# Layer norm statistics on VectorE, the last two experts one by one, and the last norm and store in halves

## The reference

```python
def layer_norm(x, g, b):
    xf = x.astype(jnp.float32)
    mu = jnp.mean(xf, axis=-1, keepdims=True)
    var = jnp.mean(jnp.square(xf - mu), axis=-1, keepdims=True)
    return ((xf - mu) * lax.rsqrt(var + EPS) * g + b).astype(x.dtype)
...
        h = layer_norm(DEEPNORM_ALPHA * h + mix, ln_g[layer, 0], ln_b[layer, 0])
        ffn = peer(h, peer_w_q[layer], peer_subkeys[layer], peer_u[layer], peer_v[layer])
        h = layer_norm(DEEPNORM_ALPHA * h + ffn, ln_g[layer, 1], ln_b[layer, 1])
```

```python
        act = jax.nn.gelu(jnp.einsum('td,ted->te', xb, u), approximate=False)
        coef = (gate * act.astype(jnp.float32)).astype(xb.dtype)
        return jnp.einsum('te,ted->td', coef, expert_v[e])
```

## Time and profile before

| | |
|---|---|
| median of 3 runs | 2472.62 us (2468.64 to 2475.14) |
| the profiled execution | 2467.16 us, of which the span of instructions is 2465.4 us |
| busy: TensorE, VectorE, ScalarE, GpSimd | 90%, 68%, 37%, 35% of the span |
| DMA | 939.16 MB, 805.36 MB of it gathers of experts |
| bandwidth in most of the stream | 425 to 427 GB/s |
| mean granted TensorE clock | 0.987 of full speed |

### The profile page before, as it was taken

The page is one execution under the profiler, slowest core; times in us unless marked ns, Lnnn a source line. Parts: engine busy times, 40 slices in busy tenths (PEclk is TensorE's granted clock), DMA queues, the critical chain, the costliest instruction groups (busy, mean ns, idle before and its releaser), DMA issues.

```text
span 2465.4 us, 29977 instructions
## 1 busy us (share of the span) xinstructions
PE 2215.2 (90%) x9826; PEld 1270.1 (52%) x9826; DVE 1664.4 (68%) x3979; ACT 915.4 (37%) x2663; POOL 874.6 (35%) x796
## 2 busy tenths in 40 slices
PE   9989999989898889999989998889999999977776
PEld 7877745545454445555545554435555545523233
DVE  3864576666665677666777667567667767777764
ACT  2232233332333434343443434434345533433332
POOL 0022044443433344433334443234333334444442
PEclk9999999999999999999999999999999999999999
DMA  5321599999999999999999999999999999999996
GB/s 206 129 70 37 225 400 425 426 426 426 426 405 423 422 394 426 425 426 424 423 414 426 426 418 425 414 425 407 425 417 403 409 426 426 421 424 427 427 426 288
DMA packets 150792, 939.16 MB, mean 381 GB/s; under 512 B 16768, under 2 KB 19040, under 8 KB 52208
## 3 DMA queue, kind: packets, MB, share of 16 engines
q0 software_dynamic: 110592, 805.36, 78.0%
q1 hardware_dynamic: 40048, 131.91, 13.8%
HBM read 936.15 MB, written 1.05 MB: 380 GB/s over the span
## 4 chain that ended last, share of the span: by engine, by line
PE 47%; DMA 35%; DVE 8%; ACT 5%; issue 4%; POOL 1%; DVEq 0%; ACTq 0%; POOLq 0%
DMA arena<-in_uv,idx 34%; PE bank L1939 27%; PE bank L373 6%; DVE arena L1967 4%; PE bank L1569 3%; PE bank L1581 2%; ACT arena L2007 1%; PE bank L848 1%; PE bank L871 1%; DMA weights<-in_sb_v 1%; PE bank L607 1%; POOL arena L2028 1%; DVE arena L1224 1%; ACT arena L1995 1%; PE bank L835 1%
## 5 line engine op out<-in xcount | busy, mean ns | idle before, releaser
L1939 PE MATMUL bank<-arena 128*128 128x512 f32 x3072 | 1427.2, 609 | 212.3 <-ACT arena L2007 197.7
L2028 POOL DMA_INDIRECT arena<-in_uv,idx x768 | 846.8, 1103 | 1373.2 <-PE bank L1939 1249.4
L1939 PEld LDWEIGHTS bank<-arena 128*128 128x128 f32 x3072 | 566.9, 193 | 907.9 <-issue 599.6
L1967 DVE CUSTOM_DVE_ANT_0 arena<-arena,h 128x1024 f32<-128x1024 f32 x512 | 627.5, 1226 | 370.8 <-DMA arena<-in_uv,idx 358.0
L1995 ACT ACTIVATE arena<-arena 128x2 f32<-128x2 f32 x384 | 78.2, 204 | 1111.4 <-DVE arena L1967 1111.1
L1967 DVE CUSTOM_DVE_ANT_0 arena<-arena 128x1024 f32<-128x1024 f32 x256 | 313.8, 1226 | 193.8 <-DMA arena<-in_uv,idx 188.8
L2007 ACT ACTIVATE arena<-const,arena 128x128 f32<-128x128 f32 x768 | 260.4, 386 | 0.0
L373 PEld LDWEIGHTS bank<-xT,weights 128*128 128x128 f32 x1616 | 227.3, 191 | 46.2 <-issue 29.1
L373 PE MATMUL bank<-xT,weights 128*128 128x128 f32 (+2 forms) x1616 | 246.0, 308 | 0.0
L2001 ACT ACTIVATE arena<-arena 128x1 f32<-128x1 f32 x768 | 184.8, 288 | 12.6
L1556 ACT ACTIVATE arena<-bank 128x128 f32<-128x128 f32 (+4 forms) x174 | 52.1, 307 | 144.5 <-PE bank L373 50.4
(11 more groups left out here) (338 smaller groups left out, 1928.3 us busy)
## 6 DMA issues: line engine op xcount, KB each, us to landing
weights<-in_w_in SPq DMA_DIRECT2D x38, 512.0 KB
weights<-in_w_q SPq DMA_DIRECT2D x30, 512.0 KB, 20.6
weights<-in_a_fm SPq DMA_DIRECT2D x28, 512.0 KB
arena<-in_uv,idx POOLq DMA_INDIRECT x768
weights<-in_a_out SPq DMA_DIRECT2D x16, 512.0 KB
weights<-in_b_fm SPq DMA_DIRECT2D x16, 512.0 KB
weights<-in_b_out SPq DMA_DIRECT2D x16, 512.0 KB
arena<-in_w_q SPq DMA_DIRECT2D x14, 512.0 KB, 14.6
```

Of the source, the lines that this page charges most:

```text
L1939: ins = nc.tensor.matmul(acc[:, :], diag[:, e % DIAGS, :], ring[:, e % RING, at:at + 512], start=first, stop=last)
L1967: V.tensor_tensor_reduce(out=u, in0=u, in1=x, scale=1.0, scalar=0.0, op0=ALU.mult, op1=ALU.add, accum_out=dots[:, unit % 2, kx:kx + 1]).th ...
L2028: nc.gpsimd.indirect_dma_start(out=ring[:, s, :], out_offset=None, in_=io[f"uv{unit // PH // NT}"], in_offset=bass.IndirectOffsetOnAxis(ap ...
```

## The change

It has four parts.

1. The statistics of a layer norm: `moments` takes the place of `mean` and the layer norm's part of `variance`. Two `bn_stats` over 512 columns each and one `bn_aggr` give mean and variance on VectorE; one instruction adds epsilon and one takes the reciprocal. `norm_squares` on ScalarE remains for the RMS norms (m = 0, 1) alone. `ln_scaled` subtracts the mean. With this the reciprocal is done at base+1 (odd norms) or base+41 (even ones) and no longer at base+2 or base+43, and ScalarE's square root is due at base+1 or base+42 and no longer at base+2 or base+43.
2. The last two experts singly: ScalarE does Gelu, coefficient and diagonal of expert 766 as soon as its dot is there, then those of expert 767. After that the table with Sqrt is loaded ahead of its use.
3. The last norm in halves (`last_norm`): TensorE signals `last_low` when the low half of expert 767 is done, and VectorE adds that half and takes its `bn_stats` before it waits for the high half. The last tile's store is two DMAs of 512 columns, each issued when its half is done.
4. The rows g and b of the last norm are spread at slot 376 and no longer after slot 383 (`WINDOW * (5 + i) - 8 * i`).

```diff
         def norm_squares(act, m, i):
-            if m > 1:
-                act.wait_ge(sem(f"ln_mean_{i}"), m - 1)
-            elif m == 1:
+            if m == 1:
...
-        def mean(v, m, i):
-            nc.vector.tensor_reduce(small[:, 4 + i:5 + i], h[:, i, :], AX.X, ALU.add).then_inc(sem("dve_step"), 1)
+        def moments(v, m, i):
+            for half in range(2):
+                half_stats(i, half).then_inc(sem("dve_step"), 1)
+            v.wait_ge(sem("dve_step"), count("dve_step", 2))
+            moments_joined(v, i)
+            nc.vector.tensor_scalar(small[:, 2 + i:3 + i], small[:, MOMENTS + 2 * i + 1:MOMENTS + 2 * i + 2], 1e-5, None,
+                                    ALU.add).then_inc(sem("dve_step"), 1)
             v.wait_ge(sem("dve_step"), count("dve_step"))
-            nc.vector.tensor_scalar(small[:, 4 + i:5 + i], small[:, 4 + i:5 + i], -1.0 / D, None,
-                                    ALU.mult).then_inc(sem(f"ln_mean_{i}"), 1)
-            v.wait_ge(sem(f"ln_mean_{i}"), m - 1)
+            v.wait_ge(sem(f"norm_var_{i}"), 2 * m)
+            nc.vector.reciprocal(small[:, 2 + i:3 + i], small[:, 2 + i:3 + i]).then_inc(sem(f"norm_var_{i}"), 1)
+
+        def half_stats(i, half):
+            at = STATS + 12 * i + 6 * half
+            return nc.vector.bn_stats(out=small[:, at:at + 6], in_=h[:, i, half * 512:(half + 1) * 512])
+
+        def moments_joined(v, i):
+            at = STATS + 12 * i
+            nc.vector.bn_aggr(out=small[:, MOMENTS + 2 * i:MOMENTS + 2 * i + 2],
+                              in_=small[:, at:at + 12]).then_inc(sem("dve_step"), 1)
+            v.wait_ge(sem("dve_step"), count("dve_step"))
...
+        def last_norm(v):
+            i = NT - 1
+            for half, acc in enumerate((acc_lo, acc_hi)):
+                if half == 0:
+                    v.wait_ge(sem("last_low"), 1)
+                else:
+                    v.wait_ge(sem("v_used"), UNITS * PK)
+                hs = h[:, i, half * 512:(half + 1) * 512]
+                nc.vector.scalar_tensor_tensor(hs, hs, ALPHA, acc[:, :], ALU.mult, ALU.add).then_inc(sem("last_added"), 1)
+                v.wait_ge(sem("last_added"), half + 1)
+                half_stats(i, half).then_inc(sem("dve_step"), 1)
+            v.wait_ge(sem("dve_step"), count("dve_step", 2))
+            moments_joined(v, i)
...
         def queries_scalar(act, n, i, base):
             yield base + 42
-            norm_squares(act, 2 * n, i)
-            yield base + 43
             norm_root(act, 2 * n, i)
...
-            mean(v, 2 * n, i)
+            moments(v, 2 * n, i)
             yield base + 43
-            variance(v, 2 * n, i)
             ln_scaled(v, 2 * n, i)
...
                                                start=first, stop=last)
+                        if half == 0 and e == UNITS * PK - 1:
+                            ins.then_inc(sem("last_low"), 1)
...
+            for j in range(GROUP):
+                e, kx = UNITS * PK - GROUP + j, PK - GROUP + j
+                act.wait_ge(sem("dots"), e + 1)
+                nc.scalar.activation(actv[:, par, kx:kx + 1], dots[:, par, kx:kx + 1], ACT.Gelu).then_inc(sem("gelu"), 1)
...
+            nc.scalar.preload_act_table_set("sqrt_and_others")
...
-                yield WINDOW * (5 + i)
+                yield WINDOW * (5 + i) - 8 * i
                 for which in range(2):
                     row_tensor(pe, 5, i, which)
...
                 if n > 1:
                     yield base + 1
-                    mean(v, 2 * n - 1, i)
+                    moments(v, 2 * n - 1, i)
                 yield base + 2
-                variance(v, 2 * n - 1, i)
                 if n > 1:
                     ln_scaled(v, 2 * n - 1, i)
+                else:
+                    variance(v, 1, i)
...
                 yield base + 1
-                norm_squares(act, 2 * n - 1, i)
-                yield base + 2
+                if n == 1:
+                    norm_squares(act, 1, i)
+                    yield base + 2
                 norm_root(act, 2 * n - 1, i)
...
-            for i in range(NT):
-                normed(sp, 5, i)
-                sp.dma_start(out[i], h[:, i, :]).then_inc(sem("out_written"), 16)
-            sp.wait_ge(sem("out_written"), 16 * NT)
+            normed(sp, 5, 0)
+            sp.dma_start(out[0], h[:, 0, :]).then_inc(sem("out_written"), 16)
+            for half in range(2):
+                f = slice(half * 512, (half + 1) * 512)
+                sp.wait_ge(*banks.emptied(("row", 5, 1, 1, half)))
+                sp.dma_start(out[1][:, f], h[:, 1, f]).then_inc(sem("out_written"), 16)
+            sp.wait_ge(sem("out_written"), 16 * (NT + 1))
```

More of the change, by code:

```diff
@@ L60 @@
 GLA_DV = 128
+SMALL = 96
+STATS = 64
+MOMENTS = 88
 MEM_H = 4
@@ L228, in build @@
         row_parts = sbuf("row_parts", [10 * KC, P])
-        small = sbuf("small", [P, 64])
+        small = sbuf("small", [P, SMALL])
         idx_best = sbuf("idx_best", [P, 2, PK], U32)
@@ L1423, in norm_squares @@
                 act.wait_ge(sem("w_o_last_added"), 2)
-            kw = {"bias": small[:, 4 + i:5 + i]} if m > 1 else {}
             junk = norm_junk if m else first_junk if i == 0 else actjunk
-            ins = nc.scalar.activation(junk, h[:, i, :], ACT.Square, accum_out=small[:, i:i + 1], **kw)
+            ins = nc.scalar.activation(junk, h[:, i, :], ACT.Square, accum_out=small[:, i:i + 1])
             ins.then_inc(sem(f"squares_{i}"), 1)
@@ L1433, in norm_root @@
                                  ACT.Sqrt).then_inc(sem(f"norm_var_{i}"), 1)
-        def mean(v, m, i):
-            nc.vector.tensor_reduce(small[:, 4 + i:5 + i], h[:, i, :], AX.X, ALU.add).then_inc(sem("dve_step"), 1)
-            v.wait_ge(sem("dve_step"), count("dve_step"))
-            nc.vector.tensor_scalar(small[:, 4 + i:5 + i], small[:, 4 + i:5 + i], -1.0 / D, None,
-                                    ALU.mult).then_inc(sem(f"ln_mean_{i}"), 1)
-            v.wait_ge(sem(f"ln_mean_{i}"), m - 1)
+        def moments(v, m, i):
[5 more added lines that the diff above has]
+                                    ALU.add).then_inc(sem("dve_step"), 1)
+            v.wait_ge(sem("dve_step"), count("dve_step"))
+            v.wait_ge(sem(f"norm_var_{i}"), 2 * m)
[8 more added lines that the diff above has]
+            v.wait_ge(sem("dve_step"), count("dve_step"))
         def variance(v, m, i):
             v.wait_ge(sem(f"squares_{i}"), m + 1)
-            ins = nc.vector.tensor_scalar(small[:, 2 + i:3 + i], small[:, i:i + 1], 1.0 / D, 1e-5 if m > 1 else 1e-6,
-                                          ALU.mult, ALU.add)
+            ins = nc.vector.tensor_scalar(small[:, 2 + i:3 + i], small[:, i:i + 1], 1.0 / D, 1e-6, ALU.mult, ALU.add)
             ins.then_inc(sem("dve_step"), 1)
@@ L1489, in ln_scaled @@
         def ln_scaled(v, m, i):
-            apply_row(v, m, i, 0, ALU.add, small[:, 4 + i:5 + i], ALU.mult)
+            apply_row(v, m, i, 0, ALU.subtract, small[:, MOMENTS + 2 * i:MOMENTS + 2 * i + 1], ALU.mult)
         def ln_apply(v, m, i):
@@ L1517, in peer_added @@
             v.wait_ge(sem("peer_added"), 2 * (w + 1))
+        def last_norm(v):
[11 more added lines that the diff above has]
+            moments_joined(v, i)
+            nc.vector.tensor_scalar(small[:, 2 + i:3 + i], small[:, MOMENTS + 2 * i + 1:MOMENTS + 2 * i + 2], 1e-5, None,
+                                    ALU.add).then_inc(sem("dve_step"), 1)
+            v.wait_ge(sem("dve_step"), count("dve_step"))
+            v.wait_ge(sem(f"norm_var_{i}"), 10)
+            nc.vector.reciprocal(small[:, 2 + i:3 + i], small[:, 2 + i:3 + i]).then_inc(sem(f"norm_var_{i}"), 1)
+            ln_scaled(v, 5, i)
+            ln_apply(v, 5, i)
         def fm_tensor(pe, m, i, src):
@@ L1993, in stream_scalar @@
                     e = unit * PK + kx
+                    if e == UNITS * PK - GROUP:
+                        break
                     act.wait_ge(sem("dots"), e + GROUP)
@@ L2012, in stream_scalar @@
                         softmax_exp(act, unit + 1)
+            for j in range(GROUP):
+                e, kx = UNITS * PK - GROUP + j, PK - GROUP + j
+                act.wait_ge(sem("dots"), e + 1)
+                nc.scalar.activation(actv[:, par, kx:kx + 1], dots[:, par, kx:kx + 1], ACT.Gelu).then_inc(sem("gelu"), 1)
+                act.wait_ge(sem("gelu"), e // GROUP + 1 + j)
+                nc.scalar.activation(coef[:, par, kx:kx + 1], actv[:, par, kx:kx + 1], ACT.Copy,
+                                     scale=gate[:, par, kx:kx + 1]).then_inc(sem("coef"), 1)
+                act.wait_ge(sem("coef"), e + 1)
+                act.wait_ge(sem("v_used"), e - DIAGS + 1)
+                nc.scalar.activation(diag[:, e % DIAGS, :], ident, ACT.Copy,
+                                     scale=coef[:, par, kx:kx + 1]).then_inc(sem("diag"), 1)
+            nc.scalar.preload_act_table_set("sqrt_and_others")
             beside.run(UNITS * PK)
```

(3 more changed lines are left out.)

## The result

The changed kernel takes 2493.8 us (median of 4 runs, 2491.44 to 2499.4), the kernel before 2470.63 us beside it. The ratio is 1.0098, with a 95% interval of 1.0083 to 1.0113: **slower by 1%**, 23 us, where 2468.2 us had been forecast. The span of the profiled execution is 2491.9 us.

What follows compares the result with a forecast made beforehand. The stream of gathers was taken to set the time from about 320 to 2448 us, with the tail unhidden. Tail 4.0 plus stream 0.4 gave 4.4 us; against the median, 2468.2 us (ratio 0.998), range 2460 to 2475.

Steps and rivals of the forecast that it cites:

- the tail: From the last dot's start to the span's end, 16.8 us with nothing hidden; the change was to save 4.0 us.
- a late start of the last dot: Sign of being wrong: expert 767's dot starting several us off 2448.6, so that the stream made the difference.
- four rivals: Stream gives back more (17%), statistics cost two passes (13%), slower (4%), rows at slot 376 hold up gathers (5%).
- The one that ended slower: Seven stream norms: added VectorE time uses up the gathers' lead, 13.4 us; 2483.9 us, 0.46% slower; chance 4%.
- Experts singly: Last two experts after the stream: the last matmul ends at 2453.13 instead of 2454.59, 1.46 us earlier, bound by TensorE.
- The two-pass rival: Layer norms: `bn_stats` takes 1.22 us, `bn_aggr` 0.5; tail gives 2.6, stream loses 2.0; 2472.0 us; chance 13%.
- The store: Last tile's output: the second half, 256 KB less, ends 0.30 us sooner after issue, between nothing and 0.61.
- is needed for the rest: Last norm's rows: spread after the stream, they would be 2.5 us late for the faster chain.
- The cover at slot 376: Gathers issue 12.6 us before their dots, so TensorE's 2.5 us of lateness there leaves 10 and costs nothing.
- A window under 420 GB/s behind slot 376: Sign of being wrong: gather bandwidth below 420 GB/s in any window after the rows are spread there.
- The stream's norms: Norms beside the gathers: 0.9 us gained in three odd ones, 0.5 lost in one even; 0.4 us gained.
- The first rival: Behind the stream's norms: shorter VectorE waits recover lost bandwidth, 4.1 us; 2464.5 us, 0.33% faster; chance 17%.

## Why the prediction was wrong

**The step that failed** is one sentence: "The 128 bytes by which tensors move cost nothing that any row shows." No row could show it, since the kernel before had the arena on a multiple of 512; that was a reason to bound the cost from both sides, and it was set to nothing. The cost is 30 us (2499.68 less 2469.04 in the kernel before, 2493.8 less 2463.56 in the changed one). It falls on 768 gathers that set the time of 86% of the span, so 1.4% of each is more than all that the tail could give. With the arena back on its boundary the whole change measures 2463.56 us against 2469.04 beside it, 5.5 us less where 4.4 was forecast. Of the signs of being wrong that the prediction names, a late start of the last dot came, by 31 us.

Of the four rivals none was this. The one that ended slower had VectorE use up the gathers' lead. The lead stands: in the changed kernel VectorE waits for the gather ahead of the last dots by 1.19 and 1.23 us, as it did before. The range, too, was drawn around mechanisms between engines and didn't hold a cost for the DMA engines' own rate.

The Trainium skill bears on it and should have been weighed: "DMA: Bandwidth & Descriptors", section "How a descriptor splits into AXI transactions". It says that a transfer is read in pieces of up to 256 bytes, each from a boundary of 256, so that the first piece of a transfer that starts off a boundary begins at the boundary below it. The runs agree with the 256: starts on a multiple of 256 or of 512 bytes cost nothing, and starts 32, 64 and 128 bytes past one do. They don't agree with the sizes. As an estimate from that section, an 8 KB row off the boundary takes 33 pieces and not 32, 3.1% more; by the skill's beats of 32 bytes a shift of 128 bytes would cost 4 beats on 256, 1.6%, and one of 32 bytes 0.4%. Measured are 1.2% and 1.5%. The skill also tells this of reads, and here it is the destination in SBUF that moved. So by which mechanism the address costs the DMA engines time stays open.

**The tail, by its own steps.** The forecast for it was 4.0 us; it gave 4.4 (16.8 to 12.36 or 12.4).

- Experts singly: 1.46 forecast, 1.47 measured. TensorE is the bound of the pair, as said; the first residual was due 3.75 us after the last dot's start and came at 3.76.
- `bn_stats`: 0.69 forecast from the row sum's slope, 0.69 measured. `bn_aggr`: 0.20 and 0.21. The two-pass rival is out.
- The square root is done at 2486.88, ahead of its use at about 2488.0; no idle time stands before `ln_apply`. The table load, 1.28 us, ends at 2483.06 with nobody waiting.
- The store: 0.30 forecast as the middle between nothing and 0.61 us, 0.6 measured. Of the tail's terms this is the mis-sized one; 0.61 us, the upper bound worked out from the bandwidth, was the right value.
- Part 4 "is needed for the rest" was wrong, and the 2.5 us with it. Of these, 1.5 us are a slip: with part 2 TensorE is done with the experts 1.47 us earlier, and the rows then start earlier too, 4.40 us after the last dot's start (before 5.87). The rest took the end of all four banks for the start of the first use. `ln_scaled` needs the first two banks, full after half of the 3.74 us, and by the time that `ln_apply` starts the last ones are full. The cover at slot 376 held: gathers were issued up to 2.1 us later, and no dot was. A window under 420 GB/s behind slot 376, which the prediction names as a sign of being wrong, comes there (415) without any loss.
- What is left of the 4.4 us after part 2 and the store, 2.4 us, is the statistics, the table load out of the path, and the first half's residual and `bn_stats` beside TensorE's high half. These three were not undone one by one.

**The stream's norms.** The mechanism was right and worth nothing. VectorE's 0.94 us in the odd norms went, as forecast; in the even ones the wait went from 2.07 to 2.45 where 2.3 was forecast (all four read 2.44 or 2.45). The sum of 0.4 us can't be told from nothing: the two kernels that differ in this alone have the same ratio. The first rival, 4 us given back, is out with it, as 4 us lie beyond the interval between these two.

## What to carry to other kernels

When a diff changes the size of a tensor, work out where the tensors behind it land, and keep the destination of the heaviest transfers on a multiple of 256 bytes. A kernel whose DMA engines are busy throughout has its time in GB/s: compare that figure first, and when it is lower in all slices at the same DMA share, look at addresses and sizes before waits. To read a tail of a few us, measure it from the last landing in the profile, where it repeats to 0.1 us (12.32 to 12.40 in five kernels with the same tail), and not by the total, which spreads over 6 to 8 us.

## What the runs showed of the hardware

- Gathers of 8 KB rows into SBUF at 427 GB/s fall to 419 to 421 when the destination starts 32, 64 or 128 bytes past a multiple of 256; other shifts were not tried. The DMA engines read fully busy either way, so the busy share doesn't tell. The profile page's row of the gather queue, before and after, gives the time of a packet: 110592 packets take 78.0% of 16 engines over 2465.4 us before, 278 ns each, and 78.2% over 2491.9 us after, 282 ns each (small packets included; the 8 KB packets alone take 312 and 316 ns).

```profile
q0 software_dynamic: 110592, 805.36, 78.0%
```

```profile
q0 software_dynamic: 110592, 805.36, 78.2%
```

- Direct loads of 4 KB rows that start 64 bytes off such a multiple lose nothing that can be measured (ratio 1.0007 when they are moved onto it). Whether that is the row's length, the queue, or that the gathers set the time and the loads don't, was not tried.
- `bn_stats` on 512 fp32 columns takes 0.69 us, so two cover 1024 columns in 1.4 us, and give the variance too, where the row sum alone takes 1.22.
- 256 KB less in the last store end it 0.6 us earlier, as long as 256 KB take at 427 GB/s.
